# A two-block network on one core: the table's units, the memory queries and the norms of the heads in another order

## What is computed

```python
h = rms_norm(x, g_mix); proj = h @ w_in                 # 4352 columns
sb_q, sb_k, sb_v, d_q, d_k, d_v, m_q = split(proj)
y_sb  = stick_breaking_attention(8 heads of 64) @ w_o_sb
y_dil = dilated_mixture(rms_norm(d_q), rms_norm(d_k), d_v) @ w_o_dil   # 3 groups x 4 heads of 64, dilations 1, 4, 16
y_mem = memory_attention(rms_norm(m_q), rms_norm(k), v) @ w_o_mem      # 4 heads of 128, k and v = mem_h @ w_mem_kv
x = x + (gates[0]*y_sb + gates[1]*y_dil + gates[2]*y_mem) @ w_out      # gates = sigmoid(h @ w_gate + b_gate)
x = x + peer_ffn(rms_norm(x))   # per token and head: top 16 of 128 x 128 experts; dot with row u, gelu, weigh row v
```

## Time and profile before

| what | value |
|---|---|
| median of 3 runs (lowest, highest) | 3061.82 us (3052.39, 3067.17) |
| the profiled execution | 3071.63 us, span 3069.9 us |
| TensorE busy | 2254.1 us, 73% of the span |
| VectorE busy | 1325.2 us, 43% |
| GpSimd busy | 807.3 us, 26% |
| ScalarE busy | 458.8 us, 15% |
| moved by DMA | 966.19 MB, 315 GB/s over the span |
| TensorE's granted clock, mean | 0.867 |

### The profile page before, as it was taken

The page is one execution under the profiler, slowest core; times in us unless marked ns, Lnnn a source line. Parts: engine busy times, 40 slices in busy tenths (PEclk is TensorE's granted clock), DMA queues, the critical chain, the costliest instruction groups (busy, mean ns, idle before and its releaser), DMA issues. The chain is left out here.

```text
span 3069.9 us, 26996 instructions
## 1 busy us (share of the span) xinstructions
PE 2254.1 (73%) x9958; PEld 1103.9 (36%) x9958; DVE 1325.2 (43%) x2719; ACT 458.8 (15%) x905; POOL 807.3 (26%) x883
## 2 busy tenths in 40 slices
PE   7946697847747556558998989888699786555554
PEld 4525333714313222225554323222264543222221
DVE  3367434779996777764642111112211441001011
ACT  1313100212210111102231300000010412000000
POOL 3323433458777777760100000000000000000000
PEclk9976798978868777779997999999999987888888
DMA  9986999799999999996543499999922354999997
GB/s 373 374 307 225 355 393 357 258 369 381 379 360 364 386 349 369 366 333 221 186 143 137 173 406 410 409 410 410 400 90 82 110 186 173 409 409 409 410 410 297
DMA packets 294470, 966.19 MB, mean 315 GB/s; under 512 B 22369, under 2 KB 23521, under 8 KB 294241
## 3 DMA queue, kind: packets, MB, share of 16 engines
q1 hardware_dynamic: 182754, 562.20, 47.2%
q0 software_dynamic: 111616, 402.71, 35.2%
HBM read 896.67 MB, written 68.16 MB: 314 GB/s over the span
## 5 line engine op out<-in xcount | busy, mean ns | idle before, releaser
L2464 PE MATMUL ps<-big 128*32 128x256 f32 (+1 forms) x4608 | 586.2, 516 | 229.1 <-DMA big<-in_moe_w_up_dram 84.7
L432 PE MATMUL ps<-big 128*128 128x512 f32 (+3 forms) x1776 | 615.2, 507 | 28.8 <-PEq L330 8.0
L1827 PE MATMUL ps<-big 128*128 128x512 f32 x512 | 329.4, 786 | 233.0 <-ACT big L1845 116.9
L432 PEld LDWEIGHTS ps<-big 128*128 128x128 f32 (+1 forms) x1776 | 336.2, 192 | 299.9 <-issue 272.4
L2464 PEld LDWEIGHTS ps<-big 128*32 128x32 f32 (+1 forms) x4608 | 219.8, 132 | 575.9 <-issue 284.5
L1880 DVE SCALAR_TENSOR_TENSOR big<-big 128x1024 f32<-128x1024 f32 x256 | 313.5, 1226 | 108.5 <-DMA big<-peer_rows,big 94.2
L1778 POOL DMA_INDIRECT big<-in_peer_v_dram,big x256 | 297.7, 1163 | 120.6 <-issue 75.0
L1771 POOL DMA_INDIRECT big<-peer_rows,big x256 | 294.5, 1150 | 99.6 <-issue 77.9
L1827 PEld LDWEIGHTS ps<-big 128*128 128x128 f32 x512 | 115.4, 243 | 411.9 <-issue 283.3
L2564 DVE TENSOR_TENSOR big<-big,ps 128x512 f32<-128x512 f32 (+1 forms) x32 | 17.7, 555 | 502.6 <-issue 368.7
L603 POOL DMA_DIRECT2D peer_rows<-big x256 | 149.5, 591 | 323.9 <-DVE big L615 301.7
(11 more groups left out here) (330 smaller groups left out, 1998.5 us busy)
## 6 DMA issues: line engine op xcount, KB each, us to landing
big<-in_moe_w_gate_dram SPq DMA_DIRECT2D x64, 2048.0 KB, 23.2
big<-in_moe_w_up_dram SPq DMA_DIRECT2D x64, 2048.0 KB, 23.5
big<-in_moe_w_down_dram SPq DMA_DIRECT2D x64, 2048.0 KB, 23.8
big<-in_peer_u_t_dram POOLq DMA_DIRECT2D x64, 1024.0 KB, 11.4
peer_rows<-big POOLq DMA_DIRECT2D x256, 256.0 KB, 6.9
big<-in_ada_w_dram SPq DMA_DIRECT2D x24, 2048.0 KB, 7.8
big<-in_mlstm_w_in_dram SPq DMA_DIRECT2D x12, 2048.0 KB, 15.6
big<-in_w_in_dram SPq DMA_DIRECT2D x8, 2048.0 KB, 20.9
```

The source lines that it names most:

```text
L432: last = pe.matmul(bank(i), lhsT, rhs, start=(j == 0), stop=(j == len(t.pairs) - 1))
L1827: last = pe.matmul(k.ps[:, 4 + 2 * t + half, :], diag[n // 2 % 4], v_buf[n % NV][:, 512 * half:512 * half + 512], start=(n < PER and n % G ...
L2464: last = pe.matmul(k.ps[q * M:q * M + M, bank, 0:W], lhsT(kc), w4[s][:, c, q * W:q * W + W], start=(kc == 0), stop=(kc == C - 1), skip_gro ...
```

## The change

- The projection weights come in the order of blocks 0, 1, 2, 7, 8, 3, 4, 5, 6: the memory queries (7 and 8) ahead of the dilated heads' columns (3 to 5).
- The norms are in three rounds: memory keys and queries behind pair 1 (between its second and third unit of the table), dilated queries behind pair 2, dilated keys at the end. Their scratch buffer is smaller and elsewhere.
- Units behind the pairs are 3, 3, 2, 2 instead of 3, 3, 3, 3. The softmax block does 2 ahead of its first scores, and none behind the eighth unit of attention; 17 instead of 16. Branches does 7 instead of 6, the merge 13 instead of 12 (one ahead of its first gate), mix_out 4. So 3 instead of 4 are left for the expert stage.
- The head turns run at the head of the softmax block (memory heads first) instead of in a block of their own; TensorE waits for all 20 to be stored before its first scores. The index is made by GpSimd at the end of the projections, and buffers of the masks move.

```diff
+PROJ_BLOCKS = (0, 1, 2, 7, 8, 3, 4, 5, 6)
...
-    tiles("proj", d["w_in"][0], 0, 4352)
+    for a in PROJ_BLOCKS:
+        tiles("proj", d["w_in"][0], 512 * a, min(512 * a + 512, 4352))
...
-    for a in range(2, 9):
+    for b, a in list(enumerate(PROJ_BLOCKS))[2:]:
...
-    ahead, each = 10, 3
+    ahead, behind_pair = 10, (3, 3, 2, 2)
...
             sb.vector(dve, g)
-            k.expert_rows.vector(dve, each)
             if g == 1:
+                k.expert_rows.vector(dve, 2)
                 norms(dve, stored, 0)
-        norms(dve, stored, 1)
+                k.expert_rows.vector(dve, 1)
+            else:
+                k.expert_rows.vector(dve, behind_pair[g])
+            if g == 2:
+                norms(dve, stored, 1)
+        norms(dve, stored, 2)
+
+    def place(pool):
+        pool.iota(k.key_place, pattern=[[P, TT], [-1, T]], base=0, channel_multiplier=1).then_inc(k.key_placed, 1)
...
-    rounds = ([(k.tok[:, t, 512:512 + nd * DIL_DIM], nd, DIL_DIM, tile_of["dil", t]) for t in range(TT)],
-              [(k.kv[:, t, 0:512], nm, MEM_DIM, tile_of["mem_k", t]) for t in range(TT)]
-              + [(k.tok[:, t, 2816:3328], nm, MEM_DIM, tile_of["mem_q", t]) for t in range(TT)])
+    rounds = ([(k.kv[:, t, 0:512], nm, MEM_DIM, tile_of["mem_k", t]) for t in range(TT)]
+              + [(k.tok[:, t, 2816:3328], nm, MEM_DIM, tile_of["mem_q", t]) for t in range(TT)],
+              [(k.tok[:, t, 512:1280], nd, DIL_DIM, tile_of["dil_q", t]) for t in range(TT)],
+              [(k.tok[:, t, 1280:2048], nd, DIL_DIM, tile_of["dil_k", t]) for t in range(TT)])
...
         @block.gpsimd
         def _(pool):
-            pool.iota(idx, pattern=[[P, TT], [-1, T]], base=0, channel_multiplier=1).then_inc(idx_made, 1)
-            k.expert_rows.pool(pool, len(units))
+            k.expert_rows.pool(pool, ROWS_FIRST + len(units) - len(without_rows))
...
         @block.tensor
         def _(pe):
+            for i, (src, _, _) in enumerate(turns):
+                if i >= 4:
+                    pe.wait_ge(head_kept, i - 3)
+                for t in range(TT):
+                    last = pe.transpose(k.ps[:, i % 4, t * P:(t + 1) * P], src[:, t, :], k.ident[:])
+                last.then_inc(head_turned, 1)
...
+            pe.wait_ge(head_kept, len(turns))
             score(0)
...
+            k.expert_rows.vector(dve, ROWS_FIRST)
             biased(0)
...
-                k.expert_rows.vector(dve, 1)
+                if i not in without_rows:
+                    k.expert_rows.vector(dve, 1)
...
+            for i, (_, dst, g) in enumerate(turns):
+                act.wait_ge(head_turned, i + 1)
+                act.activation(dst, k.ps[:, i % 4, 0:T], ACT.Identity, scale=k.col(g), bias=0.0).then_inc(head_kept, 1)
             exp(0)
...
-         rows=6)
+         rows=7)
...
         @block.vector
         def _(dve):
+            k.expert_rows.vector(dve, 1)
             for i, (half, br, t) in enumerate(order):
```

More of the change, by code:

```diff
@@ L741, in first_projections @@
                               dst=k.qkt[:, 4 * a + b, :]))
-    for a in range(2, 9):
+    for b, a in list(enumerate(PROJ_BLOCKS))[2:]:
         n = min(512, 4352 - 512 * a)
-        w = weights(k, p0 + a, n)
+        w = weights(k, p0 + b, n)
         for t in range(TT):
             at = 512 * (a - 2)
-            tiles.append(tile([(k.ht[:, c, t * P:(t + 1) * P], w[:, c, :]) for c in range(C)], n, p0 + a,
+            tiles.append(tile([(k.ht[:, c, t * P:(t + 1) * P], w[:, c, :]) for c in range(C)], n, p0 + b,
                               dst=k.tok[:, t, at:at + n]))
@@ L750, in first_projections @@
                 values = len(tiles) - 1
-            if a in (5, 8):
-                tile_of[("dil", "mem_q")[a // 8], t] = len(tiles) - 1
+            if a in (4, 5, 8):
+                tile_of[{4: "dil_q", 5: "dil_k", 8: "mem_q"}[a], t] = len(tiles) - 1
     sb = StickBreaking(k)
@@ L778, in between @@
             sb.scalar_logs(act, scores_of[i])
-    ahead, each = 10, 3
+    ahead, behind_pair = 10, (3, 3, 2, 2)
+    k.key_place = work(k, 5632, 512).bitcast(I32)
+    k.key_placed = k.sem("key_placed")
     def beside(dve, stored):
@@ L828, in head_turns @@
 def head_turns(k):
-    nc = k.nc
-    full, free = k.sem("heads_turned"), k.sem("heads_stored")
     dq = k.tok[:, :, 512:512 + 2 * DIL_HEADS * DIL_DIM]
@@ L838, in head_turns @@
     k.mkt = work(k, 15872, 1024).rearrange("p (c t) -> p c t", c=4)
-    turns = [(dq[:, :, c * P:(c + 1) * P], k.dqt[:, c, :], "gq_dil") for c in range(6)] \
-        + [(dq[:, :, 768 + c * P:768 + (c + 1) * P], k.dkt[:, c, :], "gk_dil") for c in range(6)] \
-        + [(mq[:, :, c * P:(c + 1) * P], k.mqt[:, c, :], "gq_mem") for c in range(4)] \
-        + [(mk[:, :, c * P:(c + 1) * P], k.mkt[:, c, :], "gk_mem") for c in range(4)]
-    with nc.Block(no_gpsimd_drain=True) as block:
-        @block.tensor
-        def _(pe):
-            for i, (src, _, _) in enumerate(turns):
-                if i >= 4:
-                    pe.wait_ge(free, i - 3)
-                for t in range(TT):
-                    last = pe.transpose(k.ps[:, i % 4, t * P:(t + 1) * P], src[:, t, :], k.ident[:])
-                last.then_inc(full, 1)
-        @block.scalar
-        def _(act):
-            for i, (_, dst, g) in enumerate(turns):
-                act.wait_ge(full, i + 1)
-                act.activation(dst, k.ps[:, i % 4, 0:T], ACT.Identity, scale=k.col(g), bias=0.0).then_inc(free, 1)
+    return [(mq[:, :, c * P:(c + 1) * P], k.mqt[:, c, :], "gq_mem") for c in range(4)] \
+        + [(mk[:, :, c * P:(c + 1) * P], k.mkt[:, c, :], "gk_mem") for c in range(4)] \
+        + [(dq[:, :, c * P:(c + 1) * P], k.dqt[:, c, :], "gq_dil") for c in range(6)] \
+        + [(dq[:, :, 768 + c * P:768 + (c + 1) * P], k.dkt[:, c, :], "gk_dil") for c in range(6)]
@@ L860, in softmax_attentions @@
 def softmax_attentions(k):
     nc = k.nc
-    scores, soft, turned, copied, out_full, out_done, exped, maxed, idx_made = (
-        k.sem(f"sm_{s}") for s in ("scores", "normed", "turned", "copied", "out", "stored", "exp", "max", "index"))
+    scores, soft, turned, copied, out_full, out_done, exped, maxed = (
+        k.sem(f"sm_{s}") for s in ("scores", "normed", "turned", "copied", "out", "stored", "exp", "max"))
+    head_turned, head_kept = k.sem("heads_turned"), k.sem("heads_stored")
+    turns = head_turns(k)
@@ L866, in softmax_attentions @@
     S = [work(k, at, 768) for at in (6144, 6912, 12288)]
     PT = [work(k, 9472 + 768 * b, 768) for b in range(2)]
-    idx = work(k, 7680, 512).bitcast(I32)
-    low = work(k, 6144, 512).bitcast(I32)
-    far = work(k, 6656, 512)
-    dist = work(k, 11008, 512)
+    idx = k.key_place
+    low = work(k, 19968, 512).bitcast(I32)
+    far = work(k, 20480, 512)
+    dist = work(k, 1536, 512)
+    ROWS_FIRST, without_rows = 2, (7, )
     bar = work(k, 16896, 1536)
@@ L1096, in _ @@
         def _(pool):
-            k.expert_rows.pool(pool, len(order))
+            k.expert_rows.pool(pool, len(order) + 1)
         @block.sync
@@ L2806, in two_blocks_kernel @@
                   ("proj", lambda: first_projections(k)),
-                  ("heads", lambda: head_turns(k)), ("softmax", lambda: softmax_attentions(k)),
+                  ("softmax", lambda: softmax_attentions(k)),
                   ("merge", lambda: gated_merge(k)), ("peer", lambda: peer_experts(k)),
```

8 lines of the change are left out of this document (4 added, 4 removed).

## The result

| | before | with the change |
|---|---|---|
| median (lowest to highest) | 3061.8 us (3052.4 to 3069.3, 5 runs) | 3034.0 us (3030.2 to 3042.9, 5 runs) |
| ratio, 95% interval | | 0.9918 (0.9897 to 0.9938) |
| the profiled execution, its span | 3071.6, 3069.9 us | 3042.9, 3041.1 us |
| its TensorE clock, mean | 0.867 | 0.871 |

The change is faster by 27.8 us between the medians and by 28.7 us between the profiled executions. The forecast was 3030.

What follows compares the result with a forecast made beforehand. A pipeline of 64 units paced by DMA, with two gaps made by VectorE. Terms -26.1 + 2.0 - 7.6 = -31.7 gave 3039.9 us for the profiled execution, 3030 us against the median; range 3018 to 3048.

Steps and rivals of the forecast that it cites:

- step 1: Projection block: two short TensorE waits replace the 11.7 us one, and the block ends at 202.6 instead of 230.0, -27.4 us.
- rival A: Projection block: each burst of units waits for stores, VectorE's queue slips 12 us; gain 21, 3041 us; chance 0.12.
- step 4: Merge: TensorE's clock will have fallen after a longer pause in front, +2.0 us; the 12 steps stay at 8.1 us.
- step 3: Units until the gated merge, paced by DMA: two more intervals +12.4, one beside weight loads +2, bursts +1; together -26.1 us.
- The start of the softmax block: Mask built beside the turns, two units before the scores: first unit at 210.5, 41.5 us earlier.
- Rival D: Merge: TensorE's clock stays at 1.2 GHz, 16.2 us per slow step; six such give +17, 3079 us; chance 0.04.
- The expert stage: Three units left instead of four, so selection starts earlier by 7.6 us; bounds 0 and -7.6.
- B: Expert stage keeps its start because scores or gathers hold it; gain 24, 3038 us; chance 0.07.
- C: Merge: the 13th unit makes it run at DMA pace, costing 29 us, 3059 us, no change; chance 0.04.
- The idle time per stretch: Sign, 98 to 350 us: no stretch has DMA idle over 10 us.
- TensorE's longest pause in the projections: Sign, projection block: this pause is under 4 us.
- The sign for the selection: Sign, expert stage: selection begins some 34 us earlier than 559.

Runs made afterwards that it cites:

- change_again: The changed kernel itself, unaltered, run again on chip C: median 3050.9 us, ratio 0.9929 to before.
- six_fourteen: The changed kernel with 6 units in branches and 14 in the merge instead of 7 and 13, chip B: 3024.0 us, ratio 0.9864 to before.
- unit_to_merge: The kernel before with one unit of the expert stage moved into the merge, nothing else, chip A: 3055.1 us, ratio 0.9980 to before.
- two_left: The changed kernel with 14 units in the merge and 2 instead of 3 left for the expert stage, chip B: 3038.4 us, ratio 0.9914.
- plain_six: plain_weights with 6 units in branches and 14 in the merge, chip C: 3050.7 us, ratio 0.9934 to before.
- plain_five: plain_weights with 5 units in branches and 15 in the merge, chip C: 3042.6 us, ratio 0.9905 to before.
- six_once_more: six_fourteen repeated on chip D: median 3060.4 us, ratio 0.9940 to before.
- plain_weights: The changed kernel with weights in the old order and norms as dilated queries, dilated keys, memory heads, chip A: 3029.6 us, ratio 0.9904 to before.

## Why the prediction was right

The median came out 4 us above the forecast, well inside the range, and the mechanism was the one forecast: the idle time of the DMA engines fell from 43 to 13 us, and the projection block gave the largest part. By its steps, for the profiled execution:

| step | forecast | measured, between the two traces |
|---|---|---|
| 1, end of the projections | 230.0 to 202.6: -27.4 | to 206.5: -23.5 |
| 2, first unit of the softmax block | 210.5: -41.5 | 214.18: -37.8 |
| 3, start of the 44th unit | -26.1 | 357.62: -24.7 |
| 4, merge's first tile | +2.0 | 9.92 for 7.10: +2.8 |
| 5, expert stage, with its three units | -7.6 | 27.9 - 21.8 = 6.1: -6.1 |
| sum, start of selection | -31.7 | -27.9 |

1. **The projection block** is where the sum failed most, by 3.9 us: step 1's "these two waits replace the 11.7 us one". Set against this execution's own start, 2.9 us earlier than before's (first scores at 94.3 for 97.2), the block ends even 6.8 us later than forecast. The larger part arises at pair 1, and it is rival A's mechanism on a small scale: the unit ahead of the memory round, which by the forecast would start at 139.5, or 136.6 by this start, waited for a store and started at 141.23. That the sums ahead of it took 3.6 instead of the 1.9 us forecast mattered little: in change_again, with first scores at 94.1, they took 1.9, and the unit waited 3.46 us instead of 2.12 and started at 140.6. VectorE is thus 4.5 us late at pair 2. The smaller part is the slow clock behind the wait there: the sums took 3.6 again and the next tile 8.2 instead of 7.0, 2.9 us together. The slow tile behind the first wait cost nothing, since TensorE waited for VectorE at pair 2 anyway. The forecast had a term for the slow clock only in the merge (step 4), and 1 us for the bursts only in step 3. Behind pairs 2 and 3 no unit waited. TensorE and VectorE at pair 1 in change_again:

```profile
129.91 0.49 PE L658 MATMUL ps<-big,key_after 128*128 128x128 f32 x2 [3.22 <-DVE big L710]
...
131.80 7.03 PE L434 MATMUL ps<-big 128*128 128x512 f32 x16
...
140.57 2.37 DVE L617 STREAM_TRANSPOSE big<-big 128x1024 f32<-128x1024 f32 x2 [3.46 <-DMA peer_rows<-big]
```

2. **The start of the softmax block** went as worked out: 7.1 us from the mask's start to the first unit, the turns beside it, and the first scores ready (217.0) before VectorE was through with its two units (218.7).

3. **The run of units** was mis-sized the other way: it lost 37.8 - 24.7 = 13.1 us of the lead, where 15.4 were forecast. Up to the 41st unit (332.90 for 360.79) the two more intervals cost 9.9 us instead of 12.4. The three intervals behind it, beside the weight loads, cost 3.2 more than before instead of 2. The 1 us for bursts belongs to step 1, where it was too little. The units ran at 352 GB/s, a little over the 344 that the forecast had read. The figure of the Trainium skill's DMA: Bandwidth & Descriptors (Anatomy of one DMA), 436 GB/s, does not describe this run of units. It stands nearer to the merge, where weights and units together reached 412 GB/s in six_fourteen.

4. **The merge** began with one slow tile, as forecast, for 2.8 instead of 2.0 us: the tile's 7.10 became 9.92. Rival D, a slow clock through the merge, did not occur: the second tile took 7.1 in every kernel here. That the first is slow is not certain: it took 7.10 behind before's pause of 2.83 us, 8.63 behind 2.86 in unit_to_merge, and 9.3 to 10.1 behind pauses of 4.8 to 12.1.

5. **The expert stage** gave 6.1 of 7.6 us. As before, its two first units run together (517.89 and 520.20, before 539.42 and 541.70); the last one now starts 8.57 us behind them, with 6.25 of waiting for a store, where before each of the two behind them took 7.4 to 7.6.

**The rivals.** A: the burst behind pair 1 cost some 4 us, not 11, and the one behind pair 2 nothing. B fell, since selection moved with the units; but two_left shows that it decides one unit further on. C fell for 13 units; plain_six, plain_five and six_once_more show it for 14 and 15 where the merge starts early. D fell.

**The signs.** The idle time per stretch (6.5 us at most) and the one slow tile held. That TensorE's longest pause in the projections stays under 4 us held for this trace (3.3), but not for the five others with the same projection block, which have 4.87 to 6.55. The projection block ended at 206.5 and not near 203, the first unit was at 214.2 and not at 210 to 213, the merge at 362.5 for near 360. The sign for the selection, 34 us before 559, doesn't fit the forecast's own sum of 31.7, since it leaves out step 4, and selection began at 560.66 before; it came 27.9 us earlier. The range takes 8 us at its low end and 7, called the same, at its high end.

**What was luck.** That the median is only 4 us off owes something to chance. The misses of the steps partly cancel (3.9, 0.8 and 1.5 us lost, 2.3 won back). The one trace of before was a late one: against unit_to_merge, the same program up to the merge and with first scores at 94.4 as the change's 94.3, the 44th unit is 22.4 us earlier, not 24.7, where 26.1 were forecast. And behind the gather the stages that the change doesn't touch vary by more than the miss: from the gather to the loading of the mLSTM's output weights took 951.1 us before and 944.3 with the change. The forecast's ratio, 0.9896, lies just outside the measured interval.

What the forecast could not have shown is how little of the gain belongs to the reordered weights. plain_weights has it all without them. By the traces about 19 of the 28 us come from the split round (tried without the moved units only with the reordered weights), the turns inside their user's block and the unit moved into the merge, and 9 from where the units stand. The first figure holds the late start of before's trace, the second is not seen in the medians.

**What stays open.** On chips C and D the change's first gather is as early as in the first comparison (550.7 and 548.5 us), yet the medians are 24.4 and 16.3 us below before where the first comparison had 27.8 (ratios 0.9929 and 0.9948; the intervals overlap). No trace of the kernel before was taken there, so where it is smaller, if it is, isn't settled.

## What to carry to other kernels

Look for the resource that paces the long run, find its idle holes in the stretches, and ask of each which engine's queue made it; then split the one long task that stands ahead of a waiting one, and let units of background work straddle a block's end instead of standing ahead of it. Price a short wait of TensorE with the matmuls behind it, not by its length alone, and ask of each burst of background units when the stores it needs can be through. Before a cover is loaded further, work out its limit in units: here one more unit made the cover end late in two of four traces, and part of what was won ahead of it was lost at its end. And take more than one trace of the kernel before: two traces of one program here were 2 to 4 us apart at marks that no edit had touched.

## What the runs showed of the hardware beyond what was expected

**Short pauses and TensorE's clock.** The sums behind a wait take 0.49 us for their first pair when the clock stays up and 0.80 when not. In the projection blocks here they were fast after waits of 1.06, 1.49, 1.88, 2.08, 2.09, 2.29, 3.03, 3.06, 3.17, 3.22 and 3.42 us (after 2.08, in two_left, only the first pair: the sums took 3.1 us in all, and the tile behind them 7.48), slow after 2.49, 2.95 and 3.33, and slow after all of 4.87, 5.27, 5.37, 5.53, 6.55, 6.63 and 7.12 and after the three of 10.9 to 11.8. Whether the next tile was slow too varied: 7.03 us after the wait of 4.87, 8.29 after that of 5.37. Two executions of one kernel differ in this (change and change_again at 130 us: 3.33 and 8.15 us, 3.22 and 7.03 us). The Trainium skill's TensorE: Matmul & The Clock Gate (HAM oscillation) describes pauses behind which the next burst starts on the slow clock, and the traces agree where the first pair took 0.80 us.

**The first 60 us.** From 24 to 60 us, with the same work in every kernel here, the granted clock was 0.91 in the trace of before, 0.95 in eight traces and 1.00 in five, the change's among them; TensorE's first scores lay at 97.2, at 95.8 to 96.1 and at 94.1 to 94.4 us. That is 3 us of a difference between two traces which no edit made.

**Chips.** From the first gather to the loading of the mLSTM's output weights took 933 to 944 us in the seven traces from chips A and B, and 953 to 967 in the five from C and D, with the same code, gathers of rows by index. Of before's median, C and D are 15 to 18 us above A. Kernels are to be compared on one chip.
